# First stage of a two-block kernel: two kinds of weight units mixed from the 25th on, and the squares, their sum and half of the scaling of x given to GpSimd

## What is computed

```
c_act = silu(c)
mod   = c_act @ w_ada + b_ada                        # shift, scale, gate (also for c_ctx)
u     = rms_norm(x, pre_w) * (1 + scale) + shift     # x: 512 + 256 tokens of 2048
mkv   = rmsnorm(mem, mem_norm_g[l]) @ w_mem_kv[l]    # l = 0, 1; keys and values of the memory
```

## Time and profile before

| | |
|---|---|
| median of three runs | 3540.46 us |
| the profiled execution: device time, span of its trace | 3543.83 us, 3542.0 us |
| TensorE busy over the span | 95% |
| VectorE, ScalarE, GpSimd busy | 50%, 42%, 8% |
| first stage | from 0 to about 226 us |

### The profile page before, as it was taken

How to read it: one execution, slowest core, us unless ns; L and a number is a source line. 1 busy time by engine, 2 the same in 40 slices (tenths; PEclk the granted TensorE clock), 3 DMA queues, 4 the chain that set the end, 5 groups by cost and what they waited for, 6 DMA issues and landing times.

```text
span 3542.0 us, 53287 instructions
## 1 busy us (share of the span) xinstructions
PE 3350.4 (95%) x21854; PEld 2750.7 (78%) x21854; DVE 1769.4 (50%) x2930; ACT 1480.2 (42%) x2312; POOL 298.7 (8%) x311
## 2 busy tenths in 40 slices
PE   7889999999996898789899999999999999999998
PEld 4888888888875777778677777887877777788787
DVE  7865565666624666554744444333344444433432
ACT  6564343244325344233465554222235555532221
POOL 0000230131002323200100000000000000000000
PEclk8999999999997999989999999999999999999999
DMA  9742434434532110063422222333432222233242
GB/s 364 234 138 64 129 90 133 128 109 127 159 100 105 38 50 26 14 221 96 139 74 80 83 77 88 107 95 113 148 104 86 71 81 82 82 103 98 89 149 78
DMA packets 142611, 385.44 MB, mean 109 GB/s; under 512 B 15360, under 2 KB 23680, under 8 KB 142368
## 3 DMA queue, kind: packets, MB, share of 16 engines
q1 hardware_dynamic: 133968, 352.01, 31.0%
q0 software_dynamic: 8400, 30.02, 2.7%
HBM read 351.36 MB, written 30.61 MB: 108 GB/s over the span
## 4 chain that ended last, share of the span: by engine, by line
PE 48%; DVE 2%; ACT 1%; issue 1%; DVEq 0%; DMA 0%; POOL 0%; ACTq 0%
PE lay_acc L2359 41%; PE lay_sA L2469 1%; PE lay_ob L2487 1%; PE lay_nb L2430 1%; PE lay_tb L2448 1%; PE lay_om L2359 1%; PE lay_om L2497 0%; DVEq L2837 0%; PE lay_om L2376 0%; PE lay_sA L2376 0%; DVE stream_x L2838 0%; PE lay_sB L2376 0%; PE lay_ob L2376 0%; DVE lay_room L2836 0%; DVE lay_u_lo L2973 0%
## 5 line engine op out<-in xcount | busy, mean ns | idle before, releaser
L2359 PE MATMUL lay_acc<-lay_u_hi,lay_whi 128*128 128x512 f32 x2144 | 854.1, 398 | 0.0
L2359 PE MATMUL lay_acc<-lay_u_hi,lay_wlo 128*128 128x512 f32 x2144 | 836.7, 390 | 0.0
L2359 PE MATMUL lay_acc<-lay_u_lo,lay_whi 128*128 128x512 f32 x2144 | 835.7, 390 | 0.0
L2781 DVE TENSOR_TENSOR lay_wlo<-lay_stage,lay_whi 128x1024 fp32r<-128x1024 f32 x320 | 400.1, 1252 | 600.2 <-ACT lay_whi L2572 599.2
L2572 ACT ACTIVATE lay_whi<-lay_stage 128x1024 fp32r<-128x1024 f32 x320 | 337.1, 1055 | 581.3 <-PE lay_acc L2359 415.3
L2359 PEld LDWEIGHTS lay_acc<-lay_u_hi,lay_whi 128*128 128x128 f32 x2144 | 403.6, 188 | 98.0 <-issue 16.5
L2359 PEld LDWEIGHTS lay_acc<-lay_u_hi,lay_wlo 128*128 128x128 f32 x2144 | 403.1, 188 | 86.2
L2359 PEld LDWEIGHTS lay_acc<-lay_u_lo,lay_whi 128*128 128x128 f32 x2144 | 403.8, 188 | 83.5 <-issue 2.9
L802 PE MATMUL proj_lat<-proj_u_hi,proj_whi 128*128 128x512 f32 x832 | 339.5, 408 | 8.2 <-DVE proj_wlo L1018 8.2
L802 PE MATMUL proj_lat<-proj_u_hi,proj_wlo 128*128 128x512 f32 x832 | 327.5, 394 | 0.0
L802 PE MATMUL proj_lat<-proj_u_lo,proj_whi 128*128 128x512 f32 x832 | 327.0, 393 | 0.0
(11 more groups left out here) (477 smaller groups left out, 5555.6 us busy)
## 6 DMA issues: line engine op xcount, KB each, us to landing
lay_stage<-units_dram SPq DMA_DIRECT2D x288, 512.0 KB, 3.5
tokens_unit_stage<-in_units_dram SPq DMA_DIRECT2D x212, 256.0 KB, 2.7
front_stage<-in_w_ada_dram SPq DMA_DIRECT2D x64, 512.0 KB, 5.2
front_stage<-in_w_kv_dram SPq DMA_DIRECT2D x32, 512.0 KB, 4.6
tokens_kv_out<-in_w_ada_dram SPq DMA_DIRECT2D x64, 256.0 KB, 3.1
lay_stage<-out_units_dram SPq DMA_DIRECT2D x32, 512.0 KB, 3.5
tokens_x_sb<-scr_arow SPq DMA_DIRECT2D x32, 256.0 KB, 4.5
tokens_x_sb<-in_xT_dram SPq DMA_DIRECT2D x4, 1536.0 KB, 10.3
```

The costliest lines, as they stand in the source:

```text
L2359: mm = pe.matmul(bank_of(t)[:], w[:, i % SLOTS, k, :], u[:, kt, :], start=(kt == n == 0), stop=(kt == KT - 1 and n == 2))
L2781: dve.tensor_tensor(wlo[:, g % SLOTS, :, :], stage[:, g % DEEP, :, :], whi[:, g % SLOTS, :, :].bitcast(F32), ALU.subtract)\
```

## The change

It does four things, all in `front`:

1. The order of the units is written out as a string: 24 modulation units, three times a piece of 8 memory and 11 modulation units in which they alternate and three or four modulation units end it, and a last piece of 8 memory and 7 modulation units.
2. The four x loads stand at units 20, 24, 28 and 32 (before: 10, 15, 20, 25).
3. GpSimd squares all 16 tiles of x and adds them, one square and one addition after the other, with a drain behind each; ACT's and DVE's parts of that go. PE adds over partitions at unit 57 (before: 61). DVE scales tiles 0 to 7 of x, every other unit from 64 on, and GpSimd tiles 8 to 15, once DVE has made the reciprocal.
4. `take_kv` stands two places behind a row's last unit (before: three).

The number of matmuls and of splits is the same. The order is now

```diff
-    NB, NK, LEAD, AHEAD = 2 * D // 512, LAYERS * 2 * W_MEM // 512, 4, 6
-
-    seq = [("a", b, u) for b in range(LEAD) for u in range(UN)]
-    rest = [("a", b, u) for b in range(LEAD, NB) for u in range(UN)]
-    memory = [("k", r, u) for r in range(NK) for u in range(UN)]
...
-    seq += rest[:AHEAD]
-    for n, unit in enumerate(memory):
-        seq += [unit] + rest[n + AHEAD:n + AHEAD + 1]
+    NB, NK, LEAD = 2 * D // 512, LAYERS * 2 * W_MEM // 512, 24
+    EVEN, LATE = "kakakakakakakakaaaa", "kaakaakaakakkkk"
+
+    units = {"a": iter([("a", b, u) for b in range(NB) for u in range(UN)]), "k": iter([("k", r, u) for r in range(NK) for u in range(UN)])}
+    seq = [next(units[kind]) for kind in "a" * LEAD + (NK - 1) * EVEN + LATE]
...
-    X_LOAD, XSQ_AT = 10, 30
+    X_LOAD, XVAR_AT = 20, 58
...
-    x_load_at = {X_LOAD + 5 * g: g for g in range(4)}
-    xsq_at = {XSQ_AT + 2 * k: k for k in range(KT)}
-    XVAR_AT = XSQ_AT + 2 * KT
-    scale_at = {XVAR_AT + 6 + k: k for k in range(KT)}
+    x_load_at = {X_LOAD + 4 * g: g for g in range(4)}
+    ON_POOL = range(KT // 2, KT)
+    scale_at = {XVAR_AT + 6 + 2 * k: k for k in range(KT) if k not in ON_POOL}
...
-    kv_at = {last_of["k", r] + 3: r for r in range(NK) if last_of["k", r] + 3 < NU}
+    kv_at = {last_of["k", r] + 2: r for r in range(NK) if last_of["k", r] + 2 < NU}
...
-                        pe.wait_ge(x_added, KT)
...
+                        pe.wait_ge(x_added, 1)
...
-                    if i in xsq_at:
-                        k = xsq_at[i]
-                        act.wait_ge(x_loaded[k // 4], 16)
-                        act.wait_ge(x_added, k)
-                        act.activation(xsq[:, k % 2, :], x_sb[:, k, :], ACT.Square).then_inc(x_squared, 1)
...
+            @block.gpsimd
+            def _(pool):
+                for k in range(KT):
+                    if k % 4 == 0:
+                        pool.wait_ge(x_loaded[k // 4], 16)
+                    op = pool.tensor_tensor(xsq[:, min(k, 1), :], x_sb[:, k, :], x_sb[:, k, :], ALU.mult)
+                    pool.drain()
+                    if k:
+                        op = pool.tensor_tensor(xsq[:, 0, :], xsq[:, 0, :], xsq[:, 1, :], ALU.add)
+                        pool.drain()
+                op.then_inc(x_added, 1)
+                pool.wait_ge(x_inverse, 1)
+                for k in ON_POOL:
+                    pool.tensor_tensor(x_sb[:, k, :], x_sb[:, k, :], rs[:], ALU.mult)
...
-                    if i - 1 in xsq_at:
-                        k = xsq_at[i - 1]
-                        dve.wait_ge(x_squared, k + 1)
-                        if k:
-                            dve.tensor_tensor(xsq[:, k % 2, :], xsq[:, k % 2, :], xsq[:, (k - 1) % 2, :], ALU.add)
-                        dve.drain().then_inc(x_added, 1)
...
-                        dve.reciprocal(rs[:], rs[:])
+                        dve.reciprocal(rs[:], rs[:]).then_inc(x_inverse, 1)
```

More of the change, by code:

```diff
@@ L164, in front @@
     UK, UN, DEEP, SLOTS = 2, KT // 2, 6, 4
[L165 to L173 removed]
+    NB, NK, LEAD = 2 * D // 512, LAYERS * 2 * W_MEM // 512, 24
+    EVEN, LATE = "kakakakakakakakaaaa", "kaakaakaakakkkk"
+    units = {"a": iter([("a", b, u) for b in range(NB) for u in range(UN)]), "k": iter([("k", r, u) for r in range(NK) for u in range(UN)])}
+    seq = [next(units[kind]) for kind in "a" * LEAD + (NK - 1) * EVEN + LATE]
     NU = len(seq)
+    assert NU == (NB + NK) * UN
     last_of = {(kind, b): i for i, (kind, b, u) in enumerate(seq) if u == UN - 1}
     MEM_LOAD, MSQ_AT, MVAR_AT, MHI_AT = 3, 7, 12, 15
[L180 removed]
+    X_LOAD, XVAR_AT = 20, 58
     msq_at = {MSQ_AT + q: q for q in range(4)}
     mhi_at = {MHI_AT + 2 * q: q for q in range(4)}
[L183 to L186 removed]
+    x_load_at = {X_LOAD + 4 * g: g for g in range(4)}
+    ON_POOL = range(KT // 2, KT)
+    scale_at = {XVAR_AT + 6 + 2 * k: k for k in range(KT) if k not in ON_POOL}
     rows_at = {last_of["a", b] + 5: b for b in range(NB) if last_of["a", b] + 5 < NU}
     take_at = {last_of["a", b] + 2: b for b in range(NB) if last_of["a", b] + 2 < NU}
[L189 removed]
+    kv_at = {last_of["k", r] + 2: r for r in range(NK) if last_of["k", r] + 2 < NU}
     with Phase(nc, "front") as ph:
@@ L210, in front @@
             ph.sem(n) for n in ("m_squared", "m_summed", "m_var", "m_root", "m_scaled", "m_hi", "m_lo"))
-        x_squared, x_added, x_summed, var_ready, root_ready = (ph.sem(n) for n in ("x_squared", "x_added", "x_summed", "var_ready", "root_ready"))
+        x_added, x_summed, var_ready, root_ready, x_inverse = (ph.sem(n) for n in ("x_added", "x_summed", "var_ready", "root_ready", "x_inverse"))
         row_ready, mod_turned = ph.sem("row_ready"), ph.sem("mod_turned")
@@ L295, in _ @@
                     if i == XVAR_AT - 1:
-                        pe.wait_ge(x_added, KT)
-                        pe.matmul(pst[0][:], ones[:], xsq[:, (KT - 1) % 2, 0:LAT], start=True, stop=True)
-                        pe.matmul(pst[1][:, 0:CTX], ones[:], xsq[:, (KT - 1) % 2, LAT:TOK], start=True, stop=True).then_inc(x_summed, 1)
+                        pe.wait_ge(x_added, 1)
+                        pe.matmul(pst[0][:], ones[:], xsq[:, 0, 0:LAT], start=True, stop=True)
+                        pe.matmul(pst[1][:, 0:CTX], ones[:], xsq[:, 0, LAT:TOK], start=True, stop=True).then_inc(x_summed, 1)
                 for b in range(NB):
```

## The result

The changed kernel takes 3575.47 us (median of 4 runs, 3570.26 to 3577.16) against 3540.84 us of the kernel before beside it (4 runs, 3539.02 to 3545.9): ratio 1.0092, 95% interval 1.0079 to 1.0105. It is slower by about 35 us, with 3576 forecast. The profiled execution took 3577.16 us, its span is 3575.3 us (before: 3543.83 and 3542.0).

The account below looks back on a forecast made before the run. Loads and VectorE bound the stage until 86 us, TensorE behind; 233.9 + 2.8 (row stalls) + 3 (clock) + 19.3 (scalings) = 259 us against 223.6, plus 1: +36 us, so 3576 us, range 3562 to 3592.

Parts of the forecast that it names:

- The bound: First stage: loads and VectorE set the pace until 86 us, TensorE behind; VectorE is full from 50 to 62 us.
- Part 1: New unit order in the first stage, without GpSimd's effect: last product at 206 us against 223.6, +1 us for the end.
- the order alone: First stage: starting TensorE's long memory units at unit 24 instead of 38 is worth -17 us.
- The squares that leave ScalarE are worth nothing: First stage: moving the squares off ScalarE gains nothing, as it is busy 37.65 of 56 us.
- Part 2: GpSimd's work in the first stage: each 1.81 us instruction adds 1.6 us to VectorE, turns one for one; +36 us overall.
- Each waits for one GpSimd instruction: 10 x 1.6 = 16 us: From 49 us to unit 23's split: ten two-input VectorE instructions each wait 1.6 us, moving that split to 77.5 us.
- The reciprocal: From unit 58: reciprocal ends at 12.0 us, eight scaling turns take 19.5 us more, TensorE stalls 19.3 us by unit 66.
- the clock: First stage: 3 us added for one or two TensorE starts at the lower clock.
- Squares hidden: Rival: VectorE doesn't wait, or only within its 1.3 us room per pair; -17 us, 3523 us; chance 0.17.
- half the turns: Rival: VectorE gets two instructions in per GpSimd one, 0.8 us a turn, pairs at 4.86 us; 3560 us; chance 0.16.
- late one: Rival: sum of x comes after unit 57 and TensorE waits; over 3 us per instruction, 3595 us or more; chance 0.02.
- Nothing in sum: Rival: some turns lost early, some hidden, total near 3540 us; chance 0.05.

Follow-up runs that it names:

- e3: Changed kernel with each of GpSimd's 39 instructions replaced by a memset that reads nothing, sum of squares and half of x's scaling left out: 3528.22 us.
- e5: e1 with ScalarE's squares in two buffers of their own and the running sum in a third: 3531.09 us, ratio 0.9972 to the kernel before.
- e1: Changed kernel without GpSimd's block: squares on ScalarE, additions and all 16 scalings on VectorE: 3540.49 us, ratio 0.9991 to the kernel before.
- e8: Changed kernel with each of GpSimd's instructions cut into two of 128 x 384, drains as they were: 3558.21 us.
- e2: Kernel before, old unit order and x loads, with GpSimd squaring, adding and scaling tiles 8 to 15 as in the change: 3582.29 us, ratio 1.0110.
- e9: Changed kernel with a VectorE drain behind each of the four `u_lo` subtractions: 3575.94 us.
- e4: Changed kernel with all 16 scalings on VectorE, every other unit; GpSimd only squares and adds: 3558.93 us.
- e7: Changed kernel with one tiny GpSimd multiplication (128 x 64) and a memset for it at the start: 3576.69 us.

## Why the prediction was right

The mechanism, its two places and the total came out as forecast. But that the total was hit so closely is luck: the stage was forecast to end at 260 us and ended at 251.9, and 5 us that I had given to no term came later.

- **The bound.** "Until 86 us loads and VectorE set the pace" held, and the step that followed from it as well: with no room on VectorE between 50 and 62 us, what GpSimd takes is lost at once.
- **Part 1, 207 us for the last copy.** e3, where only the order and the room on VectorE act, has it at 210.29 us: 3 us off, so the size is right; its single stalls were not taken apart. What the prediction called "the order alone" holds only while the squares are off ScalarE or have a third buffer (e5). "The squares that leave ScalarE are worth nothing" was the wrong step: I argued from its busy time, 37.65 of 56 us, but it was the ring of waits with VectorE that counted, 4.51 us per pair in e1. With that ring the order gives 5 us, not 17. The trace of the kernel before shows the ring already, at 4.04 us, and the prediction has no word of it.
- **Part 2, one turn for one instruction.** Shown by the count of 21 to 21, by e3 (without reads no turns) and by e8 (half the instruction, half the wait). For an instruction that reads two different tiles the sizes were right, 1.81 us and 1.6 for the turn: the first scaling, which starts just ahead of VectorE's split, takes 1.80 us, and a turn was 1.6 us at the scalings and 1.62 at an addition (61.16 - 58.40 - 1.14). A square, which reads one tile twice, I had priced like the rest. It takes 1.46 us where nothing is ahead of it (e2), and its turn is 1.27 us (58.40 - 55.99 - 1.14). A pair of units took (115.81 - 68.74) / 7 = 6.72 us instead of 7.26, that is 1.42 us a turn: -3.7 us over seven pairs.
- **"Each waits for one GpSimd instruction: 10 x 1.6 = 16 us"** was the term that was mis-sized most. From 61.5 to 68.7 us is 7.2 us. GpSimd started at 47.8 us, near the 49 I had, but the first five VectorE instructions didn't wait at all, and e9 shows why. That is -8.8 us. The turns not taken were taken later: units 38 and 40 came at the slow pace too (38 to 40 from 115.81 to 123.52 us, 7.7 us where TensorE's prices give 4.7).
- **The reciprocal.** Forecast: it ends 12.0 us behind the sum, and the slow stretch behind it is 19.5 us. Measured: 173.88 - 162.06 = 11.8, and 193.41 - 173.97 = 19.4 us. The 33.4 us at which TensorE was to be done with unit 66 don't follow from the terms, though: with the unit split at 12.0 + 19.5 - 2.5 = 29.0 us (its scaling comes behind it) and 2.84 us of work they make 31.9, and the sum would be 1.5 us less. Measured, the unit was split at 28.9 and TensorE was done at 33.5 us (195.52 - 162.06), because it needed 4.5 us for it at a mean clock of 0.62. So the stall of 19.3 us came out, but for a reason that no term held. The price of the scalings, 9.2 us in e4, is below the 19.3 - 6.6 = 12.7 that the terms gave; e4 also puts eight scalings on VectorE, and how the difference is shared was not measured.
- **The sum.** -8.8 - 3.7 + 3.0 make 250.5 against the measured 251.9; the 1.4 us left are within what I had put down to the clock. (The lower end of the range, 3562, lies 14 us down, where 38 turns shorter by 0.3 us make 11.) What the turns cost in all, 41.6 us, was forecast as 53.
- **The rivals.** *Squares hidden* fell with the splits at 2.48 us, *half the turns* with the pair at 6.72 instead of 4.86 us; the sum of x was no late one, since the squares ended at 125.2 us and the sum was asked for some 35 us later. *Nothing in sum* fell with the ratio.

That the 35 us of the medians is so near the 36 forecast is then two deviations that cancel: 8 us less in the stage, and 5 to 6 us later in the program that remain open and are no more than the scatter of single runs. Against the medians of the kernel before that stand beside the experiments, 3543.80 and 3542.46 us, the loss is 32 to 33 us.

## What to carry to other kernels

Before an idle GpSimd is given work, look whether it and VectorE both read two tensors in SBUF at the same time: if VectorE has no room there, each GpSimd instruction cost VectorE its own length less 0.2 us here, and taking a scaling of 946 ns off VectorE by giving it a wait of 1.6 us is a loss. GpSimd's writes without reads were free here (e3). And when an engine at two thirds of its time is called "not the limit", look for a ring of waits through a pair of buffers first: a third buffer was worth 7 us of the stage, more than the 5 us that the order gave without it. Such a ring can stand unseen in the kernel one starts from, as long as another engine is behind.

## What the runs showed of the hardware that I had not expected

- The turns don't begin by themselves. In front of an unbroken run of two-input instructions on VectorE, spaced 1.14 us, GpSimd's first instruction waited: the first square is 7.14 us long, against 1.46 in e2, where it started 0.2 us ahead of a split while VectorE was idle, and the split took 2.34 us. A copy out of PSUM that stood on VectorE just as it started (47.31 to 47.98 us in the changed kernel) did not let it in, while a drain (e9) did at once. Once begun, the turns kept going one for one without any gap on VectorE. In the changed kernel, e7 and e8 GpSimd starts at 47.84, 48.49 and 48.87 us, and the first VectorE instruction that waits is the same one each time (the third `u_lo`, at 53.65, 53.74 and 54.54 us), 1.19 or 1.20 us behind the one before it instead of 1.14. Whether that small gap let GpSimd in or was already its doing, no run shows.
- The Trainium skill (SBUF — State Buffer, SBUF: two separate sides) has the pair go to whichever starts first, for the whole instruction, and the other fully blocked. The length of a turn agrees within 0.2 us: VectorE waited 1.27 us for a square of 1.46, 1.6 us for a scaling of 1.80 and, in e8, 0.80 us for a half addition of 0.99 (the two half additions from 145.99 us on ran with VectorE idle). What doesn't agree is who goes first: GpSimd's first square is on record from 47.84 us, and VectorE's split of 47.91 us and four more went ahead of it.
- A square, both inputs the same tile, takes 1.46 us and a product of two different tiles 1.80 us at the same 128 x 768, where no VectorE instruction was ahead of them. In the turns the shortest squares and additions are on record with 1.73 and 2.07 us, so those records seem to hold some waiting.
- Clearing 128 x 1536 took 1.38 us, while VectorE's splits beside it stayed at 1218 ns.
